# Conditioning matrix streamed through the residual's buffer, its column sums on VectorE during the mixing

## The reference, cut to what matters

```python
mod = silu(c) @ ada_w[l] + ada_b[l]            # 6 x 1024: shift1, scale1, gate1, shift2, scale2, gate2
h   = rms_norm(x) * (1 + scale1) + shift1
p   = h @ w_in                                 # q, kv, mqk, mv, gates, mo, ga, gb
a, m = attention(p), mlstm(p)
x   = x + gate1 * ((sigmoid(ga) * (a @ w_attn_up) + sigmoid(gb) * (m @ w_mlstm_up)) @ w_out)
h   = rms_norm(x) * (1 + scale2) + shift2
x   = x + gate2 * moe(h)                       # 16 experts, best group, top 2
```

## Time and profile before

| | us |
|---|---|
| runs of the kernel before (median of 3) | 1731.04 (1729.79 to 1739.95) |
| the profiled execution: span from first to last instruction | 1724.8 |
| TensorE busy in it | 1506.9 (87%) |
| VectorE busy in it | 563.9 (33%) |
| ScalarE busy in it | 323.4 (19%) |
| GpSimd busy in it | 121.8 (7%) |

### The profile page before, as it was taken

One profiled execution on the slowest core, in us unless ns is written; L12 is line 12 of the kernel. 1 busy time (PEld: TensorE's weight loads), 2 busy tenths in 40 slices (PEclk: granted clock), 3 DMA queues, 4 the chain that ended last, 5 costly groups with the idle time before them and its releaser, 6 DMA issues.

```text
span 1724.8 us, 18335 instructions
## 1 busy us (share of the span) xinstructions
PE 1506.9 (87%) x5819; PEld 669.3 (39%) x5820; DVE 563.9 (33%) x1459; ACT 323.4 (19%) x809; POOL 121.8 (7%) x157
## 2 busy tenths in 40 slices
PE   4999999999983999987749999999999387999982
PEld 1544444544441333332335444454444132333330
DVE  1346432446333212111134554243642411221213
ACT  3133411200011212111132343111000121221210
POOL 1100000011101000000111000000110100000001
PEclk8999999999996999999769999999999789999996
DMA  9822111055747899999952111113563799997984
GB/s 307 338 97 98 49 49 49 13 206 173 291 142 268 268 375 379 376 388 360 322 180 98 49 49 50 49 49 108 206 224 145 292 314 381 378 354 247 310 303 165
DMA packets 160813, 366.59 MB, mean 213 GB/s; under 512 B 12433, under 2 KB 14705, under 8 KB 160753
## 3 DMA queue, kind: packets, MB, share of 16 engines
q1 hardware_dynamic: 127568, 256.26, 42.2%
q0 software_dynamic: 21664, 83.89, 12.8%
q10 hardware_dynamic: 11520, 25.70, 5.0%
HBM read 334.37 MB, written 31.46 MB: 212 GB/s over the span
## 4 chain that ended last, share of the span: by engine, by line
PE 69%; DMA 11%; SPq 5%; DVE 5%; issue 4%; ACT 2%; POOL 2%; ACTq 0%; DVEq 0%; POOLq 0%; PEldq 0%
PE bank L939 23%; PE bank L1160 14%; PE bank L929 11%; PE bank L1105 6%; PE bank L1172 6%; DMA weight_ring<-in_w_up_dram 6%; DMA regA<-in_w_up_dram 2%; SPq L428 2%; SPq L431 2%; SPq L371 2%; DMA weight_ring<-in_ada_w_dram 1%; PE bank L1152 1%; PE bank L999 1%; POOL expert_rows L558 1%; PE bank L988 1%
## 5 line engine op out<-in xcount | busy, mean ns | idle before, releaser
L939 PE MATMUL bank<-h_features,weight_ring 128*128 128x512 f32 x768 | 342.4, 599 | 3.1 <-ACT regB L674 1.9
L1160 PE MATMUL bank<-weight_ring,merged_features 128*64 128x512 f32 x960 | 227.2, 628 | 35.3 <-DMA weight_ring<-in_w_up_dram 28.2
L939 PEld LDWEIGHTS bank<-h_features,weight_ring 128*128 128x128 f32 x768 | 144.8, 192 | 182.7 <-issue 182.4
L929 PE MATMUL bank<-weight_ring,h_features 128*128 128x512 f32 (+1 forms) x512 | 196.1, 541 | 1.7 <-ACT h_features L628 1.7
L1703 DVE TENSOR_TENSOR merged_features<-bank,merged_features 64x512 f32<-64x512 f32 x44 | 30.5, 693 | 381.8 <-ACT merged_features L809 381.8
L1160 PEld LDWEIGHTS bank<-weight_ring,merged_features 128*64 128x64 f32 x960 | 73.5, 144 | 165.4 <-issue 160.8
L929 PEld LDWEIGHTS bank<-weight_ring,h_features 128*128 128x128 f32 x512 | 96.0, 190 | 97.0 <-issue 91.6
L1160 PE MATMUL bank<-h_features,merged_features 128*64 128x512 f32 x256 | 117.1, 612 | 11.0 <-DMA regA<-in_w_up_dram 10.0
L1160 PE MATMUL bank<-regA,merged_features 128*64 128x512 f32 x256 | 117.5, 614 | 0.0
L1105 PE MATMUL bank<-weight_ring,merged_features 128*128 128x512 f32 x256 | 110.4, 593 | 3.0 <-POOL merged_features L538 3.0
L1172 PE MATMUL bank<-weight_ring,merged_features 128*64 128x512 f32 x480 | 109.6, 598 | 1.6 <-DVE merged_features L1689 1.6
(11 more groups left out here) (304 smaller groups left out, 1376.1 us busy)
## 6 DMA issues: line engine op xcount, KB each, us to landing
weight_ring<-in_ada_w_dram SPq DMA_DIRECT2D x24, 2048.0 KB, 8.7
weight_ring<-in_w_gate_dram SPq DMA_DIRECT2D x22, 2048.0 KB, 21.1
weight_ring<-in_w_down_dram POOLq DMA_DIRECT2D x22, 2048.0 KB, 14.9
weight_ring<-in_w_up_dram SPq DMA_DIRECT2D x22, 2048.0 KB, 20.4
weight_ring<-in_w_in_dram SPq DMA_DIRECT2D x18, 2048.0 KB, 8.9
h_features<-in_w_gate_dram SPq DMA_DIRECT2D x10, 2048.0 KB, 17.4
regA<-in_w_up_dram SPq DMA_DIRECT2D x10, 2048.0 KB, 27.4
regB<-in_w_down_dram POOLq DMA_DIRECT2D x10, 1536.0 KB, 11.5
```

What stands on the lines that cost most here:

```text
L929: ins = te.matmul(bank[:, 0:w], hT[:, k, P * i:P * i + P], wv[:, k, :], start=(k == 0), stop=(k == KD - 1))
L939: ins = te.matmul(bank[:, :], wv[:, k, c0:c0 + P], rhs[:, k, :], start=(k == 0), stop=(k == kn - 1))
L1160: ins = te.matmul(ps[3][64 * part:64 * part + 64, :], xT[:, k, :], w[:, k, :], start=(k == 0), stop=(k == KD - 1))
```

## The change

All chunks that are not in layer 0's prologue are now taken by VectorE sums, through one buffer: `xs`. After x is normed, SyncE writes x to DRAM (`x_kept`) and waits until it is there. Then it streams twelve chunks through `xs` (`STREAM`): ada 4 to 11 of this layer (n = 0 to 7) and ada 0 to 3 of layer 1 (n = 8 to 11, in both layers). Chunk n may load when sum n - 1 is done (`mid_ready`), row block 0 of it when TensorE has read the sum before (sums 0 to 7 are made in place in row block 0, sums 8 to 11 in `regP`). When sum 11 is done, x is loaded back; VectorE waits for it ahead of w_out's results.

- Sums 0 to 6 stand at the end of VectorE's rounds s = 2, 4, ..., 14 of the first half, sum 7 in ga/ya round 0, sums 8 to 11 in the merge rounds 0, 2, 4 and 6.
- TensorE's products for them (`mod_sum`) stand at the end of its rounds s = 3, 5, ..., 15, after ya 1, and after yb 1, 3, 5 and 7. VectorE reads the result at the start of its next round (`mod_chunk`).
- The head at the end of layer 0 is gone: TensorE only transposes the parameters, VectorE adds the biases to `modn`. Instead of four ada chunks SyncE loads q, kv and mqk 0 of layer 1 there.
- `params` of the next layer are issued once x is updated, ahead of expert 2's gate weights.
- The ring's slots are dealt anew; w_out's two halves are loaded after `hmT`, the gate weights of expert 1 after gb 3, up 0 after gb 7, up 1 after w_out's products. Down weights of experts 0 and 1 are issued after yb 7, those of expert 2 after w_out's products.
- `ada_group`, `bcast` and ScalarE's `ada_row` in the router stage are gone.

In the order of the diff: the tables, SyncE's loads, TensorE's products, VectorE's sums, and SyncE's loads at the end of layer 0.

```diff
+STREAM = [(0, c) for c in range(HEAD_ADA, 12)] + [(1, c) for c in range(HEAD_ADA)]
+N_OWN = 8
+ADA_AT = {("mqk", 3): 0, ("mqk", 5): 1, ("mqk", 7): 2, ("mv", 1): 3, ("mv", 3): 4, ("mo", 1): 5, ("mo", 3): 6,
+          ("ya", 1): 7, ("yb", 1): 8, ("yb", 3): 9, ("yb", 5): 10, ("yb", 7): 11}
...
+        ada_w8 = as8(xs[:, :, :].rearrange("p i d -> p (i d)"))
+        def sum_buf(n):
+            return ada_w8[:, 0, :] if n < N_OWN else regP[:, 512 * (n % 2):512 * (n % 2) + 512]
...
+                def load_ada(n):
+                    ahead, c_ = STREAM[n]
+                    src = cols8(ada_w, DEPTH - 1 if ahead else l, 512 * c_, 512)
+                    if n:
+                        sp.wait_ge(mid_ready, n)
+                    sp.dma_start(ada_w8[:, 1:KD, :], src[:, 1:KD, :]).then_inc(ada_in, 16)
+                    if 1 <= n <= N_OWN:
+                        through(sp, "ada", n - 1)
+                    sp.dma_start(ada_w8[:, 0:1, :], src[:, 0:1, :]).then_inc(ada_in, 16)
...
+                load("mqk1")
+                load("mv")
+                load("mo")
+                wait_reg(sp, head_xn, l * NT + NT)
+                sp.dma_start(xsave.rearrange("(i p) d -> p i d", p=P), xs[:, :, :]).then_inc(x_kept, 16)
+                wait_reg(sp, x_kept, l * 16 + 16)
+                load_ada(0)
...
+                through(sp, "q", NT - 1)
+                load("ga0")
+                load_ada(1)
+                load_ada(2)
+                through(sp, "mqk", 7)
+                load("ga1")
+                load_ada(3)
+                load_ada(4)
+                through(sp, "mv", NT - 1)
+                load("ya")
+                load_ada(5)
+                load_ada(6)
+                through(sp, "mo", NT - 1)
+                load("yb")
+                load_ada(7)
+                load_ada(8)
+                through(sp, "ga", 3)
+                load("gb0")
+                through(sp, "ga", 7)
+                load("gb1")
...
+                through(sp, "ya", 7)
+                load_gate(0, 0)
+                through(sp, "hmT", NT - 1)
+                load("wo0")
+                load("wo1")
+                load_ada(9)
+                load_ada(10)
+                through(sp, "gb", 3)
+                load_gate(1, 1)
+                load_ada(11)
+                sp.wait_ge(mid_ready, len(STREAM))
+                sp.dma_start(xs[:, :, :], xsave.rearrange("(i p) d -> p i d", p=P)).then_inc(x_back, 16)
+                through(sp, "gb", 7)
+                load_up(0, 0)
+                through(sp, "wo", 2 * NT - 1)
+                load_up(1, 1)
+                with sp.If(l < DEPTH - 1):
+                    sp.wait_ge(x_upd, NT)
+                    params(nxt)
                 sp.wait_ge(pj_ready, GI[("rl", 0)] + 1)
                 load_gate(2, 2)
...
+                def mod_sum(n):
+                    pe.wait_ge(mid_ready, n + 1)
+                    bank = take("ada", n)
+                    if STREAM[n][1] in (4, 5, 10, 11):
+                        ins = te.matmul(bank[:, :], ones[:, :], sum_buf(n), start=True, stop=True)
+                    else:
+                        ins = column_sums(bank, sum_buf(n))
+                    ins.then_inc(pj_ready, 1)
...
+                def sum_ada(n):
+                    dve.wait_ge(ada_in, 32 * n + 32)
+                    acc = sum_buf(n)
+                    link(ve.tensor_scalar(acc, ada_w8[:, 0, :], cz[:, 0, 0:1], None, ALU.mult))
+                    for k in range(1, KD):
+                        link(ve.scalar_tensor_tensor(acc, ada_w8[:, k, :], cz[:, k, 0:1], acc, ALU.mult, ALU.add))
+                    ve.sem_inc(mid_ready, 1)
...
                 for s in range(16):
+                    prev = ("mqk", s - 1) if s < 9 else ("mv", s - 9) if s < 13 else ("mo", s - 13)
+                    if prev in ADA_AT:
+                        mod_chunk(ADA_AT[prev])
...
+                    if s % 2 == 0 and s >= 2:
+                        sum_ada(s // 2 - 1)
...
+                    if j % 2 == 0:
+                        sum_ada(N_OWN + j // 2)
...
+                dve.wait_ge(x_back, 16)
...
                 with sp.If(l < DEPTH - 1):
+                    wait_reg(sp, gu_ready, blocks_through(sp, E - 3))
+                    load_early(nxt, "q")
+                    load_early(nxt, "kv")
+                    wait_reg(sp, y_ready, blocks_through(sp, E - 2))
+                    load_early(nxt, "mqk0")
```

More of the change, by code:

```diff
@@ L616, in _ @@
             with act.Fori(0, DEPTH) as l:
-                def ada_row(j):
-                    bank, free = ready(act, "ada", j)
-                    ac.activation(mrow[:, j % 2, :], bank[:, :], ACT.Copy).then_inc(mrow_ready, 1)
-                    act.wait_ge(mrow_ready, j - G2_ADA + 1)
-                    act.sem_inc(free, 1)
                 wait_reg(act, mod_ready, l + 1)
@@ L1303, in _ @@
                 head_norm(0, i)
-            head_mod(0)
+            head_cols(0)
+            for j in range(HEAD_ADA):
+                dve.wait_ge(head_bc, j + 1)
+                hlink(ve.tensor_copy(modc[:, 4 * j:4 * j + 4], ps[2 + j % 2][:, 0:4]))
+                ve.sem_inc(head_read, 1)
+            head_mod(modc[:, 0:16])
             with dve.Fori(0, DEPTH) as l:
```

289 lines of the change are left out of this document (116 added, 173 removed).

## The result

The changed kernel takes 1815.3 us (median of 4 runs, 1813.9 to 1818.0), the kernel before 1730.4 beside it: a ratio of 1.049 [1.045, 1.052]. The profiled execution of it has a span of 1813.8 us, 89.0 more than before. The forecast was 1792 and its range 1755 to 1820: slower, as forecast, and by 23 us more than forecast.

What follows compares the result with a forecast made beforehand. The prediction took a string of TensorE matmuls as the bound, with VectorE level with TensorE in part of the first half. Span 1724.8 + 80.4 mixing - 19 removed = 1786, median 6.2 above: 1792 us, range 1755 to 1820.

Steps and rivals of the forecast that it cites:

- VectorE is level with TensorE from round 4 to 8: Mixing's first half: VectorE, though counted little busy, has almost no idle time there, so added sums of 6.2 us delay TensorE.
- The stepping: Round-by-round walk through the first half with seven sums added, moving its end from 237.68 to 272.1 us.
- 4.7 us of lower clock: First half: TensorE's matmuls run slower after three new waits of 4.2 us or more, adding 4.7 us.
- the 34.4: First half of the mixing, one layer: 34.4 us longer, 29.7 without the lower clock.
- 80.4: Mixing of both layers: 40.2 us longer each, from 34.4 first half, 1.1 sum 7's matmul and 4.7 merge.
- Sum 7's product, 1.1: First ga/ya round: sum 7 hidden beside a projection, only its added TensorE matmul costs, 1.1 us.
- Merge +4.7: Merge rounds: +8.0 us from waiting for sum 8 and lower clock, -3.3 from fewer matmuls; net +4.7 (0 to +8).
- Restore of x hidden: Loading x back before w_out's results: some 9 us of slack, so nothing, at worst 3 us a layer.
- The stream is late: Rival: chunks through one buffer load late, 2 us at each of 11 loads, 22 a layer: 1836 us; 10%.
- Parameters moved, -13: End of layer 0's experts: moving 14 parameter loads from ahead of expert 15's gate weights saves 13 us (0 to -13).
- Change of layer, -6: Between layers: without the four head modulation chunks VectorE combines sooner after the gather's issue, saving 6 us (-3 to -8).
- Down weights earlier, 0 (0 to -5 a layer): Experts: issuing expert 1's down weights earlier taken as nothing, at best 5 us saved a layer.

Runs made afterwards that it cites:

- e1: Changed kernel with the first half's seven sums adding only row blocks 0 and 1 of 8: 1762.1 us, ratio 1.016; first half 196.1 us.
- e5: Changed kernel with TensorE's matmul for most sums one round later, sums and loads whole: 1796.3 us, ratio 1.039; first half 216.8 us.
- e11: e5 with VectorE reading the previous sum's bank before doing the next sum, not after: 1793.3 us, ratio 1.036; first half 212.9 us.
- e9: e4 with ga/ya sums after rounds 0, 3, 5 and one more sum in the first half, after round 5: 1788.2 us, ratio 1.033.
- e2: Changed kernel loading only row blocks 0 and 1 of chunks 1 to 6, sums at full length: 1816.6 us, ratio 1.047; first half 219.8 us.
- e8: Kernel before with only layer 1's 14 parameter loads moved early, to layer 0's router stage: 1725.4 us, ratio 0.9975.
- e10: Changed kernel with the old dealing of down-weight buffers and expert 1's down weights issued only after the first expert's transposes: 1810.5 us, ratio 1.045.
- e4: Changed kernel with sums after rounds 2, 8, 10, 14 and ga/ya rounds 0, 2, 4, 6, merge products a round later: 1776.9 us, ratio 1.024.

## Why the prediction was right, and where it was wrong

- *VectorE is level with TensorE from round 4 to 8* was right, and so the sign and the place. The stepping gave waits of 5.0, 4.2, 1.5, 1.1 and 7.4 us; the trace has 5.10, 3.86, 1.49, 0.76 and 7.37. The end of the first half was forecast at 272.1 and came at 272.43. (Sum 6's end stands there as 269, where its terms make 268.4; it came at 268.3.) e1 shows that it is VectorE's time; e5 and e11 together that about a fifth of it at least was the order of the products and reads, which I had not separated.
- *4.7 us of lower clock* was the mis-sized term of that sum: 10.1 us measured. That the 34.4 fits all the same is luck: I took waits and products together as 29.7 us, and they are 25.3, so two errors of some 5 us cancel. The same term is short later on: +1.7 us at w_out's products (56.87 against 55.20, behind the same wait of 1.49), where I had counted nothing. e9, where they take 55.20 again, has 104.2 from w_out to the experts, 1 to 2 us less than in the others. Over both layers the mixing came out 9.3 us above its 80.4: 0.9 in the first halves, 3.3 in the ga/ya stretches, 0.8 in the merges, 4.2 from w_out to the experts.
- *Sum 7's product, 1.1*: the stretch grew by 2.6; 1.2 of it lies ahead of ga 0 already (7.0 us from rT to it instead of 5.8), which I had not counted. *Merge +4.7*: 4.9 and 5.3. The wait of 4.69 us and its cause are as forecast, and e5 removes both: 85.8 to 78.6, 7.2 us against the 8.0 of that term.
- *Restore of x hidden*: right. It was issued at 480.20 us, and VectorE read w_out's first bank at 493.60, when TensorE had it ready. It landed in 7.7 us; the 17 us that the prediction allowed for beside GpSimd's down weights did not come, as those were issued only at 484.56, when most of it was over.
- *The stream is late*, a rival at 10%: fell for the changed kernel, by e2. VectorE did wait for a chunk, 5.40 us at sum 6, but TensorE did not wait for that sum.
- *Parameters moved, -13*: the step that failed. The 11 us in front of expert 15 were real and the move shortened them by 5.6 us, but the weights of the experts ahead come at the DMA engines' rate (376 GB/s at a share of 1.05, the windows above), so what is not waited for at one expert is waited for at another: layer 0's stage gained 2.5 us, and e8, the same step alone, 1.1 there and 5.6 in the whole. I had read a wait off one place and taken it off the total. The words "the loads ahead ran saturated" stand in the prediction, with 0 as the end of the range, and I took the other end.
- *Change of layer, -6*: -1.7. Combining did come 6 us earlier against the gather; q did not follow, being 2.8 us earlier against it. What it waited for after that I have not settled: the stretch varies between 63 and 68 us among changed kernels that are alike in it.
- *Down weights earlier, 0 (0 to -5 a layer)*: wrong in sign for layer 1, +4.6 in the stage, of which e10 gives 3.9 back. That a load which comes earlier could cost was in none of my bounds.

In one line: of the 28 us by which the sum was too low (89 against 61), some 18 are gains that did not come, the 4.6 of the down weights among them, and 9 are surcharges of the mixing, of which 3.4 are w_out's slow products. So the time stands 5 us inside the range by another way than the range was made: its upper end of 1820 was for sums fully on the path, while in fact the mixing came out near its forecast and the gains did not.

## What to carry to other kernels

An engine that is busy for a third of the span can be the bound where work is to be added, and idle pieces as long as the new work are no proof of room: ask who waits for the engine's next instruction, a round later too. A wait for weights in a stage that runs at the DMA engines' rate is not worth its length; the stage is. And when a wait is removed by moving the instruction, look whether the same wait stands at the next user of its bank.

## What the runs showed of the hardware that I had not expected

TensorE's lower clock came behind waits much shorter than the 4.2 us from which I counted it, and its cost did not go by their length. Behind 1.49 us of waiting at 204.21 and the sum's eight products of one column each (1.39 us) a projection took 10.15 us instead of 7.11, more than behind 3.86 (8.66) or 5.10 (7.90). Nor does the place decide. In layer 1 of the changed kernel the same sum's wait is 1.66 and the projection takes 8.81. In e4 the same wait costs nothing in layer 0 (2.04, then 7.03 us) and 1.7 us in layer 1 (2.03, then 8.70). And w_out's products behind their wait of 1.49 take 56.9 us in both layers of every changed kernel but e9, whose row is that of the kernel before:

```profile
472.91 55.20 PE L1131 MATMUL bank<-weight_ring,merged_features 128*128 128x512 f32 x128 [1.49 <-POOL merged_features L579]
```

What decides it these runs do not show. The windows of the projection at 205.46 (columns as in the earlier trace rows) show the clock at its lower level of 1.2 GHz, 0.50, and then back at 2.4:

```profile
205.40:209.40 4.00, 4.00 (x6) 1.89 (x7) 1.48 (x9) 2.85 (x11) 0.00 (x0) 0.50 0.94 314
209.40:213.40 4.00, 4.00 (x8) 1.54 (x7) 1.57 (x6) 1.20 (x4) 0.00 (x0) 0.73 0.55 209
213.40:217.40 4.00, 4.00 (x21) 2.15 (x20) 0.68 (x3) 0.60 (x1) 0.00 (x0) 1.00 0.00 0
```

In the first half of the changed kernel a wait of TensorE cost half as much again (19.3 us of waits, 10.1 us of slow products), and that is how I would count it, as a surcharge on the sum of the waits and not place by place. And GpSimd's product of 128x512 took 1.6 to 1.9 us and its addition 1.3 to 1.6 beside a busy VectorE, which in turn lost 40% on its multiply-adds.
